# A decoder layer on one core: gate products as two fp32r passes, and one tile's expert search ahead of the others

## The chip, the cores and the metric

The kernel runs on one core of one Trainium2 chip. The metric is the device time of one execution in microseconds (us); smaller is better. The time before is the median of three executions.

## What is computed

One decoder layer on 512 tokens of width 1024: a gated convolution beside a gated linear recurrence, a cross-attention into 256 memory tokens, and a channel mixer that looks up experts by product keys (PEER). The change is in the last part:

```python
q = (tokens @ w_query).reshape(Ntok, PEER_HEADS, 2, PEER_DK)
s = jnp.einsum('nhpd,hpkd->nhpk', q, sub_keys).astype(jnp.float32)
s_top, i_top = lax.top_k(s, K)                       # K = 16 of 128 keys, twice per head
cand = (s_top[:, :, 0, :, None] + s_top[:, :, 1, None, :]).reshape(Ntok, PEER_HEADS, K * K)
best, pos = lax.top_k(cand, K)                       # 16 experts per head and token
gate = jax.nn.softmax(best, axis=-1)
...
u = jnp.take(expert_down, idx, axis=0)               # 128 x 128 = 16384 experts
a = jax.nn.gelu(jnp.einsum('nd,nhkd->nhk', xb, u), approximate=False)
v = jnp.take(expert_up, idx, axis=0)
y = jnp.einsum('nhk,nhkd->nd', gb * a, v)
```

## The kernel before

The 512 tokens are four tiles of 128. Everything is written out by hand, engine by engine; semaphores alone set the order between engines, and each engine works through its own list in order. All large products run in fp32r, a form of float32 that TensorE takes in one pass at less precision. To keep the precision, each operand is split into an upper half (rounded to fp32r) and a lower half (the rest), and three products are summed (`three`, lines 1064 to 1066: high by high, low by high, high by low). Plain float32 products need no split.

Weights come in blocks of 128 x 1024 floats (512 KB) through a ring of four slots. SyncE loads a slot when `block_used` says that it is free; ScalarE rounds it to `w_high` (`high`, line 441); GpSimd subtracts to get `w_low` (`low`, line 347); TensorE uses it (`columns`).

The expert search and the experts go as follows:
- Queries (blocks 68 to 83): 16 blocks of `w_query`, each 24 products of 512 columns (all four tiles), then the keys (line 1287), 64 float32 products of 128 columns. Ahead of them the four tiles are normalised and transposed (lines 696, 702, 1050, 435, 709).
- Tile 3 (`ST`, the sparse tile) fetches its 128 experts per token row by row: GpSimd gathers rows of `expert_down` (line 362), VectorE takes the dot products (`dots`, line 865), and later rows of `expert_up` are added in the same manner (lines 394, 982).
- Tiles 0 to 2 (the dense tiles) compute all 16384 hidden values instead: `first_product`, 128 blocks of 24 products with 384 columns, with gelu on ScalarE (line 610) and the result stored to `hid_dram`. A map of gates, zero but for the chosen experts, then multiplies them, and `second_product` goes over all of `expert_up`.
- The top-k runs on VectorE (`top16` and the lines after it): first for tile 3, then for tiles 0, 1, 2. Meanwhile TensorE computes `first_product` blocks ahead: 72 of them (`AHEAD`) before the gate map starts. `TURN_AT` says after which block TensorE transposes a tile's choices (line 1329), `EXP_AT` after which block ScalarE takes the exponentials (line 632).
- The gate map is made in 48 steps of 8 tokens. VectorE writes one-hot matrices (`hots`: line 953 the first, line 959 the second, already multiplied by the gate); TensorE multiplies them, 8 float32 products of 128 columns per step (`gate_step`, line 1301); ScalarE copies the two banks into `stage` (line 648), and every 8 steps 4 MB go to `gate_dram`. TensorE does one `first_product` block ahead of each step. After the 48 steps 8 blocks are left.

## Time and profile before

| | |
|---|---|
| median of 3 executions | 1727.39 us (1723.75 to 1734.52) |
| profiled execution | 1726.1 us, its span 1724.4 us |
| TensorE busy | 1666.0 us, 97% of the span |
| VectorE, ScalarE, GpSimd busy | 1148.7, 723.8 and 833.1 us |
| mean granted TensorE clock | 0.991 |

The profile is of one execution. The span is the time between the first and the last recorded instruction; the execution's own time is 1.7 us longer. Matmuls overlap in the record, so the time that one product costs in a row of them is the distance between two starts, not its duration.

### The profile page before, as it was taken

Reading aid. Unit: us, or ns where it says so; the run is one execution under the profiler, and the core shown is the slowest. Engines: PE = TensorE matmul, PEld = TensorE weight load, DVE = VectorE, ACT = ScalarE, POOL = GpSimd, SP = SyncE. Lnnn points to the kernel's source line nnn. Section 1 sums busy time; section 2 is a strip of 40 time slices with the busy share of each in tenths; the row PEclk is TensorE's granted clock in tenths of the full one; section 3 lists DMA queues with packets and bytes.
Section 4 is the critical chain, followed back from the end, with each engine's and each line's share of the span. In section 5 each row is a group of like instructions: output and inputs, shape, how many; then the busy total and the mean of one; then the engine's idle time right before and its main releaser. Section 6 shows DMA issues by size and latency. Waiting matters only on the chain.

```text
span 1724.4 us, 25526 instructions
## 1 busy us (share of the span) xinstructions
PE 1666.0 (97%) x8649; PEld 1478.4 (86%) x8649; DVE 1148.7 (67%) x2255; ACT 723.8 (42%) x973; POOL 833.1 (48%) x483
## 2 busy tenths in 40 slices
PE   7999999999999999999999999988999999999998
PEld 5788787867789999999999999987788888888886
DVE  4154562131104979989798888854788887887887
ACT  5342433342324445353455555543333333333333
POOL 3362374314343677878666666655333323433340
PEclk9999999999999999999999999998999999999999
DMA  4222243213223578888788999999999999999994
GB/s 171 86 98 74 74 141 115 86 39 114 77 94 96 171 262 285 282 279 281 271 283 312 335 344 341 341 338 374 359 353 360 343 356 350 339 370 342 349 333 153
DMA packets 150697, 421.26 MB, mean 244 GB/s; under 512 B 14576, under 2 KB 71920, under 8 KB 149744
## 3 DMA queue, kind: packets, MB, share of 16 engines
q1 hardware_dynamic: 93472, 232.29, 39.7%
q0 software_dynamic: 36864, 134.23, 21.5%
q10 hardware_dynamic: 20304, 54.04, 8.0%
q8 instruction: 27, 0.44, 0.1%
q14 instruction: 30, 0.25, 0.0%
HBM read 368.08 MB, written 52.43 MB: 244 GB/s over the span
## 4 chain that ended last, share of the span: by engine, by line
PE 81%; DMA 7%; DVE 5%; ACT 2%; issue 2%; POOL 2%; ACTq 0%; SPq 0%; DVEq 0%; POOLq 0%
PE psum L1064 25%; PE psum L1065 24%; PE psum L1066 24%; DMA arena<-down_rows,kept 4%; PE psum L1301 3%; POOL w_low L347 2%; DMA arena<-hid_dram 1%; DMA arena<-up_in 1%; DVE arena L959 1%; PE psum L1268 1%; PE psum L1287 1%; DVE hT_low L779 1%; DVE hT_high L778 1%; DMA kept<-down_in 1%; PE psum L1244 1%
## 5 line engine op out<-in xcount | busy, mean ns | idle before, releaser
L347 POOL TENSOR_TENSOR w_low<-kept,w_high 128x1024 fp32r<-128x1024 f32 x212 | 520.3, 2456 | 496.5 <-ACT w_high L441 495.9
L1064 PE MATMUL psum<-hT_high,w_high 128*128 128x384 f32 (+1 forms) x1408 | 502.7, 357 | 12.3 <-POOL w_low L347 8.0
L1065 PE MATMUL psum<-hT_low,w_high 128*128 128x384 f32 (+1 forms) x1408 | 494.8, 351 | 0.0
L1066 PE MATMUL psum<-hT_high,w_low 128*128 128x384 f32 (+1 forms) x1408 | 494.8, 351 | 0.0
L441 ACT ACTIVATE w_high<-kept 128x1024 fp32r<-128x1024 f32 x212 | 224.7, 1061 | 203.3 <-DMA kept<-front_w 76.7
L1064 PE MATMUL psum<-up_high,wgt_high 128*128 128x512 f32 x768 | 300.6, 391 | 7.9 <-DVE wgt_low L995 7.6
L1065 PE MATMUL psum<-up_low,wgt_high 128*128 128x512 f32 x768 | 299.8, 390 | 0.0
L1066 PE MATMUL psum<-up_high,wgt_low 128*128 128x512 f32 x768 | 299.7, 390 | 0.0
L1064 PEld LDWEIGHTS psum<-hT_high,w_high 128*128 128x128 f32 x1408 | 266.7, 189 | 30.2 <-POOL w_low L347 9.7
L1066 PEld LDWEIGHTS psum<-hT_high,w_low 128*128 128x128 f32 x1408 | 266.2, 189 | 15.5
L1065 PEld LDWEIGHTS psum<-hT_low,w_high 128*128 128x128 f32 x1408 | 266.6, 189 | 14.8 <-issue 0.5
L445 ACT ACTIVATE up_high<-arena 128x1024 fp32r<-128x1024 f32 x128 | 135.9, 1062 | 325.1 <-DMA arena<-up_in 319.6
L865 DVE CUSTOM_DVE_ANT_0 arena<-arena,psum 128x1024 f32<-128x1024 f32 x128 | 153.3, 1211 | 77.4 <-DMA arena<-down_rows,kept 77.4
L974 DVE TENSOR_TENSOR up_low<-arena,up_high 128x1024 fp32r<-128x1024 f32 x128 | 156.6, 1223 | 56.5 <-ACT up_high L445 55.5
L1064 PEld LDWEIGHTS psum<-up_high,wgt_high 128*128 128x128 f32 x768 | 144.7, 188 | 41.4 <-issue 11.5
L394 POOL DMA_INDIRECT kept<-up_in,kept x64 | 90.7, 1417 | 167.2 <-DVE kept L982 151.4
L1066 PEld LDWEIGHTS psum<-up_high,wgt_low 128*128 128x128 f32 x768 | 144.7, 188 | 30.2
L1065 PEld LDWEIGHTS psum<-up_low,wgt_high 128*128 128x128 f32 x768 | 144.7, 188 | 29.6
L394 POOL DMA_INDIRECT arena<-up_in,kept x64 | 92.9, 1452 | 154.5 <-DVE kept L982 153.3
L610 ACT ACTIVATE arena<-psum 128x384 f32<-128x384 f32 x128 | 62.8, 491 | 200.2 <-PE psum L1066 195.2
L362 POOL DMA_INDIRECT arena<-down_rows,kept x128 | 125.1, 978 | 26.7 <-issue 16.0
L959 DVE TENSOR_SCALAR arena<-psum,arena 128x128 f32<-128x128 f32 x384 | 126.5, 402 | 0.0
(185 smaller groups left out, 1931.1 us busy)
## 6 DMA issues: line engine op xcount, KB each, us to landing
kept<-down_in SPq DMA_DIRECT2D x128, 512.0 KB, 5.0
arena<-up_in SPq DMA_DIRECT2D x128, 512.0 KB, 6.1
kept<-front_w SPq DMA_DIRECT2D x84, 512.0 KB, 3.2
hid_dram<-arena ACTq DMA_DIRECT2D x128, 192.0 KB, 4.7
gate_dram<-arena ACTq DMA_DIRECT2D x6, 4096.0 KB, 15.3
arena<-gate_dram SPq DMA_DIRECT2D x32, 768.0 KB, 7.6
arena<-hid_dram SPq DMA_DIRECT2D x128, 192.0 KB, 7.1
kept<-x_in ACTq DMA_DIRECT2D x4, 512.0 KB, 5.2
```

The source lines that it names most:

```text
L347: nc.gpsimd.tensor_tensor(w_low[:, s, :], ring[:, s, :], w_hi[:, s, :].bitcast(F32), ALU.subtract).then_inc(low_ready, 1)
L362: nc.gpsimd.indirect_dma_start(ring[slot], None, down_rows, bass.IndirectOffsetOnAxis(idx3[:, k:k + 1].bitcast(U32), 0))\
L394: nc.gpsimd.indirect_dma_start(rows_c[k % RING_C], None, up_rows, bass.IndirectOffsetOnAxis(idx3[:, k:k + 1].bitcast(U32), 0))\
L441: nc.scalar.activation(w_hi[:, s, :], ring[:, s, :], ACT.Copy).then_inc(high_ready, 1)
L445: nc.scalar.activation(up_hi[:, s, :], uraw[:, s, :], ACT.Copy).then_inc(up_high, 1)
L610: nc.scalar.activation(hid[s % 2], psum[:, 4 + s % 2, 0:DN], ACT.Gelu).then_inc(gelu_out, 1)
L865: nc.vector.tensor_tensor_reduce(ring[slot], ring[slot], h_row, 1.0, 0.0, ALU.mult, ALU.add, dot3[:, k:k + 1]).then_inc(dot_done, 1)
L959: ins = nc.vector.tensor_scalar(hot[:, s, 1, j % TB * P:(j % TB + 1) * P], iota_ps, hkT[:, 1, j:j + 1], hkT[:, 2, j:j + 1], ALU.is_equal, ...
L974: nc.vector.tensor_tensor(up_lo[:, s, :], uraw[:, s, :], up_hi[:, s, :].bitcast(F32), ALU.subtract).then_inc(up_low, 1)
L1064: nc.tensor.matmul(out, lhs[0], rhs[0], start=first, stop=False)
L1065: nc.tensor.matmul(out, lhs[0], rhs[1], start=False, stop=False)
L1066: return nc.tensor.matmul(out, lhs[1], rhs[0], start=False, stop=last)
```

## The change

Two things are changed, and some counts with them.

The gate map: the second one-hot matrix is still multiplied by the gate, but is written as fp32r, so it holds the gate's upper half. ScalarE makes a third matrix from it with the ratio of lower to upper half (`hot_lows`, eight scaled copies of 128 x 128 per step), and each float32 product becomes two fp32r products that add up in one bank. The rings of one-hot matrices go from 3 to 2. ScalarE copies the result to `stage` in another order of its elements: the writes go in runs of 4, the reads from PSUM at a stride. VectorE computes the ratio for each dense tile in five small operations.

The sparse tile: its residual, norm and transposes come first; its queries are 16 blocks of 8 plain float32 products of 128 columns, straight from the ring with no halves. The 16 blocks are then loaded a second time and used for the three dense tiles, 24 products of 384 columns each. The sparse tile's keys come behind the first of these blocks, and its top-k runs on VectorE during the others. `AHEAD` goes from 72 to 60, so 20 blocks are left behind the gate steps. The dots in a step go from 2 and 1 alternating to 1.

```diff
+RAW0, RAW = 68, 16
+USED = FRONT + RAW
-EXP_AT = (12, 28, 48, 68)
-TURN_AT = (12, 36, 56, 72)
+EXP_AT = (16, 36, 56)
+TURN_AT = (20, 40, 60)
-HOTS = 3
+HOTS = 2
-DOTS_STEP = (2, 1, 2, 1, 2, 1)
+DOTS_STEP = (1, 1, 1, 1, 1, 1)
-FIRST_GATHER = 18
+FIRST_GATHER = 4
...
@@ scalar, in a gate step @@
+            def hot_lows(n, s):
+                act.wait_ge(hot_ready, n + 1)
+                for j in range(TB):
+                    ins = nc.scalar.activation(hot[:, s, 2, j * P:(j + 1) * P], hot[:, s, 1, j * P:(j + 1) * P].bitcast(F32),
+                                               ACT.Copy, scale=hkT[:, 3, n * TB + j:n * TB + j + 1])
+                ins.then_inc(hot_low, 1)
...
             for n in range(STEPS):
+                hot_lows(n, n % HOTS)
                 early_at(AHEAD + n)
...
-                        stage[:, c % 2, :, m % 16 * 4:(m % 16 + 1) * 4].rearrange("p i n -> p n i"),
-                        psum[:, m % 3, :].rearrange("p (n i) -> p n i", i=P), ACT.Copy).then_inc(gate_out, 1)
+                        stage[:, c % 2, :, m % 16 * 4:(m % 16 + 1) * 4],
+                        psum[:, m % 3, :].rearrange("p (n i) -> p i n", n=4), ACT.Copy).then_inc(gate_out, 1)
@@ vector @@
+            dve.wait_ge(ks_out, 4)
+            choose(score[:, ST, :], sparse_k, 0, (0, 0, 0, 0), (0, 0, 0, 0), 0, 0)
+            nc.vector.scalar_tensor_tensor(idx3.bitcast(U32), sparse_k.hk[:, 0, :], float(NK), sparse_k.hk[:, 1, :],
+                                           ALU.mult, ALU.add).then_inc(idx_ready, 1)
...
+            for n in range(DT):
+                kd = choose(score[:, n, :], dense_k, kd, DOTS_SCORES[n], DOTS_CAND, DOTS_HOT[n], n)
+                gates_of(dense_k, hk[:, 2, :], n + 2)
+                step(nc.vector.tensor_copy(ghigh, hk[:, 2, :]))
+                step(nc.vector.tensor_tensor(glow, hk[:, 2, :], ghigh.bitcast(F32), ALU.subtract))
+                step(nc.vector.tensor_scalar(gden, ghigh.bitcast(F32), 1e-30, None, ALU.max))
+                step(nc.vector.reciprocal(gden, gden))
+                nc.vector.tensor_tensor(hk[:, 3, :], glow, gden, ALU.mult).then_inc(hk_ready, 1)
@@ tensor @@
-            turned_columns(ffnn, 68, 4)
+            for q in range(RAW):
+                pe.wait_ge(wt[q % 4], 16 * ((RAW0 + q) // 4 + 1))
+                for k in range(KC):
+                    ins = nc.tensor.matmul(psum[:, 2 + q // 4 % 2, q % 4 * P:(q % 4 + 1) * P], ring[:, q % 4, k * P:(k + 1) * P],
+                                           hT_s[:, k, :], start=(k == 0), stop=(k == KC - 1), skip_group_check=True)
+                ins.then_inc(block_used, 1)
...
             def gate_step(n, h):
-                pe.wait_ge(hot_ready, n + 1)
+                pe.wait_ge(hot_low, n + 1)
...
-                        ins = nc.tensor.matmul(psum[:, (2 * h + m) % 3, j % 4 * P:(j % 4 + 1) * P],
-                                               hot[:, h % HOTS, 1, j * P:(j + 1) * P], hot[:, h % HOTS, 0, j * P:(j + 1) * P],
-                                               start=True, stop=True)
+                        nc.tensor.matmul(gate, hot[:, h % HOTS, 1, j * P:(j + 1) * P], hot[:, h % HOTS, 0, j * P:(j + 1) * P],
+                                         start=True, stop=False, skip_group_check=True)
+                        ins = nc.tensor.matmul(gate, hot[:, h % HOTS, 2, j * P:(j + 1) * P],
+                                               hot[:, h % HOTS, 0, j * P:(j + 1) * P], start=False, stop=True,
+                                               skip_group_check=True)
```

On TensorE, the head of the queries before: all four tiles are transposed (`ffn_h` counts normalised tiles), then the first block follows at 512 columns.

```order
L1050 MATMUL psum<-kept,arena 128x128 [waits block_used,ffn_h]
L1050 MATMUL psum<-kept,arena 128x128 x3
L1050 MATMUL psum<-kept,arena 128x128 [waits ffn_h]
...
L1064 MATMUL psum<-hT_high,w_high 128x512 [waits ffn_ready,low_ready,ffn_h]
L1065 MATMUL psum<-hT_low,w_high 128x512
```

The same place in the changed kernel: line 1352 transposes the sparse tile alone, line 1362 is its queries (one block in two rows), and behind 16 such blocks the dense tiles' first block begins.

```order
L1352 MATMUL psum<-kept,arena 128x128 [waits block_used,ffn_sparse_h]
L1352 MATMUL psum<-kept,arena 128x128 x7
L1362 MATMUL psum<-arena,kept 128x128 [waits ffn_sparse_ready,weight_slot0]
L1362 MATMUL psum<-arena,kept 128x128 [waits ffn_sparse_ready] x7
L1362 MATMUL psum<-arena,kept 128x128 [waits weight_slot1]
L1362 MATMUL psum<-arena,kept 128x128 x7
...
L1142 MATMUL psum<-hT_high,w_high 128x384 [waits low_ready,ffn_ready]
L1143 MATMUL psum<-hT_low,w_high 128x384
L1144 MATMUL psum<-hT_high,w_low 128x384
```

The raw blocks wait for the loads alone (`weight_slot`), the dense ones for ScalarE's and GpSimd's halves as well.

On ScalarE, one gate step before: gelu and its store, the two copies to `stage`, the rounding of the block that comes two blocks later.

```order
L610 ACTIVATE arena<-psum 128x384 [waits hid_stored0,block_used]
L612 DMA hid_dram<-arena 128x384 [waits gelu_out]
L648 ACTIVATE arena<-psum 128x4x128 [waits gate_done] x2
L441 ACTIVATE w_high<-kept 128x1024 [waits weight_slot3,block_used]
```

One gate step on ScalarE in the changed kernel:

```order
L667 ACTIVATE arena<-psum 128x384 [waits hid_stored0,block_used]
L669 DMA hid_dram<-arena 128x384 [waits gelu_out]
L708 ACTIVATE arena<-psum 128x128x4 [waits gate_done] x2
L695 ACTIVATE hot<-hot,arena 128x128 [waits hot_ready]
L695 ACTIVATE hot<-hot,arena 128x128 x7
L459 ACTIVATE w_high<-kept 128x1024 [waits weight_slot3,block_used]
```

The eight scaled copies stand between the copies to `stage` and the rounding, and they wait for VectorE's one-hots.

## Rows read from the trace of the kernel before

**Rows 1.** The page: busy time by engine, and TensorE's granted clock in 40 slices.
```profile
PE 1666.0 (97%) x8649; PEld 1478.4 (86%) x8649; DVE 1148.7 (67%) x2255; ACT 723.8 (42%) x973; POOL 833.1 (48%) x483
...
PEclk9999999999999999999999999998999999999999
```

**Rows 2.** Who waited for whom: us in total, times, longest us.
```profile
DVE arena L865 <- DMA arena<-down_rows,kept: 77.4, 22, 11.5
...
PE psum L1301 <- DVE arena L959: 8.1, 7, 2.0
```

**Rows 3.** TensorE in order of time, queries: start, duration (us), operation.
```profile
430.63 1.32 PE L1050 MATMUL psum<-kept,arena 128*128 128x128 f32 x8 [1.54 <-DVE arena L696]
...
435.08 0.77 PE L1064 MATMUL psum<-hT_high,w_high 128*128 128x512 f32 x1 [1.01 <-DVE hT_low L709]
...
526.04 14.45 PE L1287 MATMUL psum<-arena 128*128 128x128 f32 x128
540.25 0.42 PE L1064 MATMUL psum<-hT_high,w_high 128*128 128x384 f32 x1
```

**Rows 4.** TensorE in order of time: fp32r products of 256, then of 384 columns.
```profile
232.75 0.28 PE L1065 MATMUL psum<-memT_low,w_high 128*128 128x256 f32 x1
...
237.19 0.28 PE L1066 MATMUL psum<-memT_high,w_low 128*128 128x256 f32 x1
...
861.58 0.34 PE L1066 MATMUL psum<-hT_high,w_low 128*128 128x384 f32 x1
...
865.25 0.33 PE L1066 MATMUL psum<-hT_high,w_low 128*128 128x384 f32 x1
```

**Rows 5.** TensorE in order of time: plain float32 products of 128 and 64 columns.
```profile
167.17 0.44 PE L1180 MATMUL psum<-arena 128*128 128x128 f32 x2
167.45 0.56 PE L1185 MATMUL psum<-arena 128*128 128x64 f32 x4
167.84 0.44 PE L1180 MATMUL psum<-arena 128*128 128x128 f32 x2
```

**Rows 6.** TensorE's weight loads in order of time, behind an idle array.
```profile
267.52 0.19 PEld L1064 LDWEIGHTS psum<-w_high,hT_high 128*128 128x128 f32 x1 [0.70 <-issue]
267.62 0.19 PEld L1065 LDWEIGHTS psum<-w_low,hT_high 128*128 128x128 f32 x1
```

**Rows 7.** Groups by line: busy us, mean ns, idle before and its releaser.
```profile
L1301 PE MATMUL psum<-arena 128*128 128x128 f32 x768 | 94.2, 276 | 8.1 <-DVE arena L959 8.1
```

**Rows 8.** VectorE in order of time: top-k of tile 3, first dots, first one-hots.
```profile
541.16 0.29 DVE L891 COPY psum<-kept 128x128 f32<-128x128 f32 x1 [97.79 <-ACT arena L600]
...
595.25 1.23 DVE L946 TENSOR_TENSOR psum<-arena 128x1024 f32<-128x1024 f32 x1
...
618.09 1.22 DVE L865 CUSTOM_DVE_ANT_0 arena<-arena,psum 128x1024 f32<-128x1024 f32 x1 [6.69 <-DMA arena<-down_rows,kept]
...
847.24 1.22 DVE L953 TENSOR_TENSOR arena<-arena,psum 128x1024 f32<-128x1024 f32 x1 [7.08 <-ACT arena L637]
```

**Rows 9.** One source line: ns min/median/max, first and last start, forms.
```profile
L940 DVE TENSOR_TENSOR arena<-arena x3: 1016/1695/2674, 679.3 to 838.5; 128x128 f32<-128x128 f32 x3
...
L632 ACT ACTIVATE arena<-arena x4: 310/310/312, 592.7 to 831.5; 128x128 f32<-128x128 f32 x4
```

**Rows 10.** ScalarE in order of time, one gate step.
```profile
883.46 0.49 ACT L610 ACTIVATE arena<-psum 128x384 f32<-128x384 f32 x1 [2.21 <-PE psum L1066]
...
884.36 2.03 ACT L648 ACTIVATE arena<-psum 128x512 f32<-128x512 f32 x2 [0.41 <-PE psum L1301]
886.18 1.08 ACT L441 ACTIVATE w_high<-kept 128x1024 fp32r<-128x1024 f32 x1
889.40 0.49 ACT L610 ACTIVATE arena<-psum 128x384 f32<-128x384 f32 x1 [2.15 <-PE psum L1066]
```

**Rows 11.** DMA issues: KB each, us to landing.
```profile
kept<-front_w SPq DMA_DIRECT2D x84, 512.0 KB, 3.2
```

More of the change, by code:

```diff
@@ L87, in build @@
             w_half, up_half = (w_hi, w_low), (up_hi, up_lo)
+        with ExitStack() as over:
+            over.enter_context(nc.sbuf_tensor("pad_hot", [P, 92 * KB], F32))
+            hot = over.enter_context(nc.sbuf_tensor("hot", [P, HOTS, 3, TB * P], F32R))
         kept = ctx.enter_context(nc.sbuf_tensor("kept", [P, 44 * KB], F32))
@@ L366, in _ @@
             k = 0
-            for i in range(16, AHEAD + 2):
+            for i in range(4, AHEAD + 2):
                 low(FRONT + i, i % 4)
@@ new lines, in _ @@
+            step(nc.vector.tensor_tensor(h_row, hn[:, ST, :], ffn_row, ALU.mult))
+            dve.wait_ge(pk_out, 4 * DT)
+            kd = 0
+            for n in range(DT):
+                kd = choose(score[:, n, :], dense_k, kd, DOTS_SCORES[n], DOTS_CAND, DOTS_HOT[n], n)
[5 more added lines that the diff above has]
+                nc.vector.tensor_tensor(hk[:, 3, :], glow, gden, ALU.mult).then_inc(hk_ready, 1)
@@ L1095, in rows @@
                 if tile_done is not None:
-                    steps = [(j, n) for n in range(len(banks)) for j in range(2)]
+                    steps = [(j, n) for n in order for j in range(2)]
                 for j, n in steps:
@@ L1100, in rows @@
                                 k0 + j == 0, k0 + j == KC - 1)
-                    if tile_done is not None and j == 1 and n < len(banks) - 1:
+                    if tile_done is not None and j == 1 and n != order[-1]:
                         ins.then_inc(tile_done, 1)
@@ L1209, in _, with product @@
                 keys(32 + b, b)
-            def product(lhs, b0, done, first, parts=None):
+            def product(lhs, b0, done, first, order, parts=None):
                 for hf in range(2):
```

358 lines of the change are left out of this document (212 added, 146 removed).

## The prediction

> **What bounds the kernel now.** I read the page's busy times first [rows 1]. TensorE is busy for 1666.0 of 1724.4 us and its granted clock is full in nearly every slice; the next engine, VectorE, stands at 67%. The 58 us that TensorE sits idle is all that better order could ever win. So I ask two things of every edit: what it adds to or takes from TensorE's own list, and whether it opens a gap there. The waits [rows 2] show how small the gaps around the change are: in the whole gate stage TensorE waited 8.1 us for one-hots, though VectorE waited 77.4 us for gathered rows. That the sparse tile's top-k (55 us on VectorE, from 541.16 to 596.5 [rows 8]) now runs during the queries gains nothing by itself, since TensorE worked through it.
>
> The sums are made against the profiled execution, 1726.1 us (span 1724.4 plus 1.7 outside); the median of the three runs is 1727.4, so the two agree.
>
> **Prices of a product.** In a row of products the price is the distance between starts. fp32r: 37 products of 256 columns take 237.19 - 232.75 = 4.44 us, 0.120 each; 21 of 384 columns take 865.25 - 861.58 = 3.67 us, 0.175 each [rows 4]. The line through both gives 0.230 at 512 columns and 0.065 at 128. Plain float32: each product is two records, and six records stand in 167.84 - 167.17 = 0.67 us, 0.112 each, although four of the six have only 64 columns [rows 5]. So the price there does not fall with the columns; something per record holds it at 0.112. A candidate: behind an idle array, with nothing to wait for, two fp32r weight loads start 0.10 us apart [rows 6]. Each product has its own weight load, so I read a load of 128 columns as taking 0.10 to 0.11 us, for fp32r too.
>
> **Queries.** Before, TensorE's part runs from 429.1 (430.63 less the wait of 1.54) to 540.25, 111.2 us: waits of 1.54 and 1.01, transposes, 16 blocks, and the keys from 526.04 [rows 3]. The blocks at 0.230 x 24 x 16 make 88.3 us of the 91.0 between 435.08 and 526.04; the rest is the slow clock behind the wait (the first product there lasts 0.77 us), which I take to come again. After: sparse queries 16 x 8 products x 2 records x 0.112 = 28.7 us; dense queries 16 x 24 x 0.175 = 67.2. Keys and transposes are as many as before. 28.7 + 67.2 - 88.3 = **+7.6 us**, all on the path.
>
> The gaps at that place: the sparse tile's norm now starts while the last three tiles' products still run, which can save most of the 2.6 us of waits [rows 3]. But behind the last raw block TensorE needs halves of the first dense block. Its slot comes free three raw blocks (3 x 16 x 0.112 = 5.4 us) before, and the load takes 3.2 [rows 11], the rounding 1.1 [rows 10] and GpSimd's low half about twice that, some 6.7 in all with 1.3 to 3 us of waiting. Together **+1 us**, between -2 and +5. The raw blocks also need 512 KB every 1.8 us. A slot is refilled in 3.2 us [rows 11] and has 5.4, so I take 0; if transfers that overlap take twice as long, a slot is 1 us late in each round of four blocks and the end is +8.
>
> **Gate products.** Before: 768 records [rows 7], 16 a step, 16 x 0.112 = 1.79 us; with the 24 products of a block 4.20 this makes the step of 889.40 - 883.46 = 5.94 that ScalarE's rows show [rows 10]. After: 16 fp32r products of 128 columns a step. No row has fp32r below 256 columns. The array time would fall, but the number of weight loads stays at 16. With the load as the floor the price is between 0.107 and the 0.120 of 256 columns; I take 0.115, near the float32 row, as the overhead of an fp32r product looks a little larger: 16 x 0.003 x 48 = **+2 us**, between -4 and +6. That is the step on which most hangs: the expected gain of one pass instead of two for each record is not there, because the loads bind.
>
> **ScalarE in a step.** It was idle 2.15 of 5.94 us [rows 10] and gets eight scaled copies of 128 columns. From below, 1.08 us per 1024 columns gives 0.13 each, 1.1 in all; from above, the 0.31 of a lone operation of that size [rows 9] gives 2.5. The two copies to `stage` take 2.03 us for 2 x 512 elements [rows 10]; they write at a stride now and will write runs of four, so I expect them cheaper, not dearer. I take 1.6, and the engine is then full at some 90%. It costs nothing while this cover holds; each 0.1 us beyond it costs 4.8 us over 48 steps.
>
> **VectorE ahead of the gates.** Before, three dense tiles took from 596.5 to 840.2 (847.24 less 7.08), 243.7 us, with waits for rows such as the 6.69 in it [rows 8]. New are 15 small operations; one of that size took 0.3 us alone and 1.0 to 2.7 us beside GpSimd [rows 9]; at 0.75 they make 11, and gathers that start earlier give 2 back: 253. TensorE has 60 blocks x 4.2 = 252 us there, so the two finish together, where VectorE had been 7 us early. Then the first step waits for a copy, one-hots and now scaled copies (0.6 + 3.8 + 2) with one block of 4.2 beside it. I take **+3 us** for both, between 0 and +19.
>
> **Waits in the gate stage.** VectorE has 1 dot a step for 1.5, so 5.1 us of work in 5.9; and four gathered rows last four steps (24 us) instead of 2.7 (16). Most of the 8.1 us goes [rows 2]: **-5 us**, between -8 and 0. Two one-hot buffers instead of three cost nothing while VectorE has this slack. The 20 blocks left behind the steps are the same work in another place.
>
> **The sum.** 1726.1 + 7.6 + 1 + 2 + 3 - 5 = **1735 us**; its bounds are 1726 + 7.6 - 2 - 4 - 8 = 1720 and 1726 + 7.6 + 5 + 8 + 6 + 19 = 1772, the last with all of them at once.
>
> **Rivals.** *Faster: the loads hide.* If the distance of the two loads is not the load's, the price falls on the line to 0.065, and 16 products cost 1.05 us. The step cannot go below VectorE's 5.1, so it ends near 5.25: 0.7 x 48 = 33 us less than before, 35 less than forecast, 1700 us. For it: the line through two widths is straight to 256 columns. Against it: the 64-column row and the two loads. The Trainium skill (TensorE: Matmul & The Clock Gate, section on the back-to-back issue gap) gives about 81 ns a product for a stream of loads and products at 128 columns; by that the gates would be an estimated 23 us cheaper than before. Its page FP8 and Floating Point Precision (section TensorE Precision Notes) counts four passes for true FP32 and a plain truncation for the reduced form, which speaks for this rival as well; no row here shows it at 128 columns.
>
> *Slower: a narrow fp32r product costs as much as a full float32 one.* The kernel used fp32r only from 256 columns up, and nothing shows that the one-pass rate holds below. If each of the 16 then costs the two records of a float32 product, 0.224, a step grows by 16 x 0.112 = 1.79 us: 86 us over 48 steps, 1735 - 2 + 86 = 1819. It decides as soon as the price is over 0.15 (+30 us).
>
> *Slower: ScalarE becomes the bound.* If the scaled copies cost over 0.27 each, or the strided read from PSUM makes the `stage` copies dearer, the step is ScalarE's. At 0.3 to 1.0 us over, 1750 to 1783. In the same group stands VectorE coming late at each of the three turns.
>
> *It does nothing.* The sparse tile's move would only matter if its top-k had been on the path; that is in the forecast.
>
> **How the numbers follow.** The forecast has 0.60, the hidden loads 0.14, the dear narrow product 0.12, ScalarE or VectorE as the bound 0.14. About 1% (17 us) is what a measurement of this kernel can tell from no change: 1710 to 1745. The forecast lies within it for 0.48 of its 0.60, above for 0.10, below for 0.02. The hidden loads are faster for 0.12 and land within for 0.02; the other two are slower. Faster 0.14, same 0.50, slower 0.36. For 8 in 10 the range runs from 1702, most of the way to the hidden loads, to 1780, which takes in nearly all of the ScalarE case and leaves the dear product out.
>
> **What would show it.** Starts of the gate products 0.11 to 0.12 us apart, with weight loads back to back, and a step of about 6.0 us; 0.065 or 0.22 would be the first two rivals. TensorE idle before the step's fp32r products with ScalarE's copies as releaser would be the third. The queries should take 28.7 and 67 us, with a gap of 1 to 3 us between. The waits for one-hots should be gone but for the first.

## The result, and the profile after

| | before | changed |
|---|---|---|
| median of four timed runs, same chip, us | 1725.57 | 1751.37 |
| ratio | 1 | 1.014, 95% interval 1.009 to 1.019 |
| profiled execution, us | 1726.1 | 1749.39 |
| its span, us | 1724.4 | 1747.7 |
| TensorE's mean granted clock in it | 0.991 | 0.989 |

The change costs 26 us by the medians and 23.3 us by the two profiled executions. It is slower by 1.4%, clear of the noise of these runs. The page of the changed kernel, busy time by engine and the granted clock, answers to [rows 1]:

```profile
PE 1679.7 (96%) x8908; PEld 1504.2 (86%) x8908; DVE 1164.7 (67%) x2268; ACT 785.0 (45%) x1356; POOL 828.7 (47%) x483
...
PEclk9999999999999999999999999899999999999999
```

TensorE is busy for 13.7 us more and stands 68.0 us instead of 58.4. Who TensorE waited for (us in total, times, longest us), where [rows 2] had 8.1 us for VectorE's one-hots:

```profile
PE psum L1142 <- POOL w_low L367: 14.7, 13, 7.5
PE psum L1142 <- DVE wgt_low L1073: 12.3, 11, 4.9
...
PE psum L1410 <- ACT hot L695: 7.8, 6, 3.0
```

The one-hots are gone from the list. In their place stand ScalarE's scaled copies with nearly the same sum, and GpSimd's low halves with 14.7 us, where the same wait of before had 8.0. Not all of the 14.7 us lies behind the gate steps: the same view of the stretch behind them alone gives, before and then changed,

```profile
PE psum L1064 <- POOL w_low L347: 4.8, 1, 4.8
```

```profile
PE psum L1142 <- POOL w_low L367: 10.4, 10, 7.5
```

To place the 23.3 us I cut both executions at the same events of TensorE's list. The moved blocks are taken out at 4.17 us each, TensorE's pace for 24 products of 384 columns:

| stretch | before | changed | change |
|---|---|---|---|
| start to the end of attention | 429.1 | 425.3 | -3.8 |
| queries and keys, to the first first-product block | 111.15 | 118.25 | +7.1 |
| to the first gate product, without its 72 (60) blocks | 10.7 | 11.4 | +0.7 |
| first to last gate product, 48 steps | 290.0 | 292.7 | +2.7 |
| to the last first product, without its 8 (20) blocks | 6.7 | 15.7 | +9.0 |
| wait before the second product | 5.0 | 5.1 | +0.1 |
| second product to the end | 538.1 | 545.7 | +7.6 |

The first and the last stretch run the same instructions in both kernels. Over all fourteen profiled kernels of this study the first ends between 423.7 and 429.1 us, and the last takes 538.1 to 548.9 us; a repeat of nearly the old kernel (e6 below) has 546.6 there. The profiled execution of before has the longest first stretch of the fourteen and the shortest last one. So I take those two rows as scatter, and three rows are left to explain: +7.1, +2.7 against a forecast of -3, and +9.0 against a forecast of nothing.

**Queries.** TensorE in order of time at the turn from the sparse queries to the dense ones, for [rows 3]:

```profile
457.28 0.94 PE L1362 MATMUL psum<-arena,kept 128*128 128x128 f32 x7
461.00 0.41 PE L1142 MATMUL psum<-hT_high,w_high 128*128 128x384 f32 x1 [2.78 <-POOL w_low L367]
...
532.80 11.00 PE L1395 MATMUL psum<-arena 128*128 128x128 f32 x96
```

The 256 records of line 1362 start between 426.6 and 457.9, with 24 records of the other tiles' transposes among them (2.6 us), and behind them TensorE waits 2.78 us for GpSimd's low half of the first dense block.

**Gate products.** TensorE in order of time, the first of one step's eight pairs:

```profile
887.41 0.22 PE L1410 MATMUL psum<-hot 128*128 128x128 f32 x1
887.47 0.27 PE L1412 MATMUL psum<-hot 128*128 128x128 f32 x1
887.58 0.27 PE L1410 MATMUL psum<-hot 128*128 128x128 f32 x1
887.69 0.28 PE L1412 MATMUL psum<-hot 128*128 128x128 f32 x1
887.80 0.28 PE L1410 MATMUL psum<-hot 128*128 128x128 f32 x1
```

They start 0.11 us apart, as the float32 records of [rows 7] did (0.112). ScalarE in the same step, for [rows 10]:

```profile
881.64 0.49 ACT L667 ACTIVATE arena<-psum 128x384 f32<-128x384 f32 x1 [1.36 <-PE psum L1144]
...
882.55 0.60 ACT L708 ACTIVATE arena<-psum 128x512 f32<-128x512 f32 x1 [0.41 <-PE psum L1412]
883.38 0.60 ACT L708 ACTIVATE arena<-psum 128x512 f32<-128x512 f32 x1 [0.23 <-PE psum L1412]
883.88 2.44 ACT L695 ACTIVATE hot<-hot,arena 128x128 fp32r<-128x128 f32 x8
886.22 1.05 ACT L459 ACTIVATE w_high<-kept 128x1024 fp32r<-128x1024 f32 x1
887.60 0.49 ACT L667 ACTIVATE arena<-psum 128x384 f32<-128x384 f32 x1 [0.33 <-PE psum L1144]
```

The step takes 887.60 - 881.64 = 5.96 us; by the starts of TensorE's gate products an undisturbed step of before takes 5.95. The eight scaled copies take 2.44 us, and in front of the next gelu ScalarE waits 0.33 us where it waited 2.15 before. The two copies to `stage` cost 0.60 each where they cost about 1.0 before.

That is the quiet step. Five steps behind the stores of the gates are not quiet. ScalarE in order of time at one of them, and TensorE:

```profile
918.51 1.06 ACT L459 ACTIVATE w_high<-kept 128x1024 fp32r<-128x1024 f32 x1 [2.40 <-DMA kept<-down_in]
920.01 0.49 ACT L667 ACTIVATE arena<-psum 128x384 f32<-128x384 f32 x1 [0.44 <-DMA hid_dram<-arena]
...
921.89 2.44 ACT L695 ACTIVATE hot<-hot,arena 128x128 fp32r<-128x128 f32 x8
...
924.46 0.32 PE L1410 MATMUL psum<-hot 128*128 128x128 f32 x1 [1.13 <-ACT hot L695]
```

VectorE had its one-hots ready: in the whole gate stage of the changed kernel ScalarE never waited for them. It came late to the scaled copies because its own list stood for a block and for a small store of `hid_dram`, which had been issued at 906.08 behind the 4 MB store and landed 13.9 us later.

**Behind the steps.** GpSimd in order of time:

```profile
1125.81 2.39 POOL L367 TENSOR_TENSOR w_low<-kept,w_high 128x1024 fp32r<-128x1024 f32 x1
1128.36 0.95 POOL L382 DMA_INDIRECT arena<-down_rows,kept  x1 [0.16 <-issue]
1129.61 0.94 POOL L382 DMA_INDIRECT arena<-down_rows,kept  x1 [0.31 <-DVE kept L930]
1130.57 2.42 POOL L367 TENSOR_TENSOR w_low<-kept,w_high 128x1024 fp32r<-128x1024 f32 x1
1133.15 0.95 POOL L382 DMA_INDIRECT arena<-down_rows,kept  x1 [0.16 <-issue]
```

A low half and two gathers, one behind the other on one engine, take 1130.57 - 1125.81 = 4.76 us, and TensorE eats a block in 4.17. Shortly before, behind the sixth store, the same list stands still:

```profile
1105.78 2.41 POOL L367 TENSOR_TENSOR w_low<-kept,w_high 128x1024 fp32r<-128x1024 f32 x1
1116.09 0.95 POOL L382 DMA_INDIRECT arena<-down_rows,kept  x1 [7.90 <-DVE kept L930]
...
1120.04 2.36 POOL L367 TENSOR_TENSOR w_low<-kept,w_high 128x1024 fp32r<-128x1024 f32 x1
```

A gather waits there for the buffer of a row that VectorE has not summed yet, because VectorE stood 14.2 us, until 1114.59, for a row to land. The rounded half of the next block is ready at 1116.4, but its low half starts only at 1120.04, behind the gathers.

### The profile page after: what moved, and what is told of

Same layout as the page of the kernel before. It is cut to its first block, busy times and chain, and to the rows that moved or that the text cites. A ratio compares the mean times of both kernels' runs of the same rounds, so it can differ in the third digit from the quotient of the medians.

```text
span 1747.7 us, 26507 instructions
## 1 busy us (share of the span) xinstructions
PE 1679.7 (96%) x8908; PEld 1504.2 (86%) x8908; DVE 1164.7 (67%) x2268; ACT 785.0 (45%) x1356; POOL 828.7 (47%) x483
## 4 chain that ended last, share of the span: by engine, by line
PE 51%; issue 20%; POOL 12%; DMA 11%; ACT 3%; DVE 2%; SPq 0%; ACTq 0%; POOLq 0%; DVEq 0%
PE psum L1142 16%; PE psum L1144 16%; PE psum L1143 16%; POOL w_low L367 10%; DMA arena<-hid_dram 4%; DMA hid_dram<-arena 3%; DMA arena<-down_rows,kept 2%; PE psum L1410 2%; PE psum L1412 2%; POOL arena L382 2%; ACT hot L695 1%; DMA arena<-up_in 1%; DMA kept<-down_in 1%; PE psum L1395 1%; ACT w_high L459 1%
## 5 line engine op out<-in xcount | busy, mean ns | idle before, releaser
L1142 PE MATMUL psum<-hT_high,w_high 128*128 128x384 f32 (+1 forms) x1408 | 495.9, 352 | 18.1 <-POOL w_low L367 14.7
L1144 PE MATMUL psum<-hT_high,w_low 128*128 128x384 f32 (+1 forms) x1408 | 488.5, 347 | 0.0
L1143 PE MATMUL psum<-hT_low,w_high 128*128 128x384 f32 (+1 forms) x1408 | 488.3, 347 | 0.0
L382 POOL DMA_INDIRECT arena<-down_rows,kept x128 | 125.4, 979 | 34.7 <-issue 12.8
L1037 DVE TENSOR_SCALAR hot<-psum,arena 128x128 fp32r<-128x128 f32 x384 | 126.6, 402 | 0.0
```

Source lines behind the costliest of these rows:

```text
L382: nc.gpsimd.indirect_dma_start(ring[slot], None, down_rows, bass.IndirectOffsetOnAxis(idx3[:, k:k + 1].bitcast(U32), 0))\
L1037: ins = nc.vector.tensor_scalar(hot[:, s, 1, j % TB * P:(j % TB + 1) * P], iota_ps, hkT[:, 1, j:j + 1], hkT[:, 2, j:j + 1], ALU.is_equal, ...
L1142: nc.tensor.matmul(out, lhs[0], rhs[0], start=first, stop=False)
L1143: nc.tensor.matmul(out, lhs[0], rhs[1], start=False, stop=False)
L1144: return nc.tensor.matmul(out, lhs[1], rhs[0], start=False, stop=last)
```

## The experiments

All ratios are to the kernel before, run on the same chip beside it; its median there was 1723.0 to 1725.9 us. "Stage" is the time from the first to the last gate product; "clock" is TensorE's mean granted clock in it, 1.00 being full speed. e4, e6, e8 and e11 leave the lower half of the gates out, e9 and e10 leave out parts of the map; they are there to measure, not to use.

| run | median us | ratio, 95% | stage us | clock |
|---|---|---|---|---|
| before | 1725.6 | 1 | 290.0 | 1.00 |
| changed | 1751.4 | 1.014 (1.009 to 1.019) | 292.7 | 0.98 |
| e1_gates_only | 1761.9 | 1.022 (1.018 to 1.026) | 324.1 | 0.93 |
| e2_sparse_only | 1729.4 | 1.003 (1.000 to 1.005) | 281.5 | 1.00 |
| e3_gathers_earlier | 1764.5 | 1.024 (1.020 to 1.027) | 326.9 | 0.93 |
| e4_upper_alone | 1734.4 | 1.006 (1.004 to 1.009) | 276.6 | 0.94 |
| e5_two_buffers | 1723.0 | 0.998 (0.996 to 1.000) | 289.7 | 1.00 |
| e6_two_fp32r | 1727.3 | 1.001 (0.998 to 1.003) | 290.6 | 1.00 |
| e7_paced | 1733.7 | 1.005 (1.003 to 1.007) | 286.6 | 1.00 |
| e8_upper_three_buffers | 1717.0 | 0.994 (0.992 to 0.997) | 262.4 | 0.96 |
| e9_small_stores | 1713.3 | 0.994 (0.992 to 0.997) | 283.9 | 0.99 |
| e10_half_columns | 1743.9 | 1.010 (1.007 to 1.014) | 293.3 | 0.94 |
| e11_upper_dots_sooner | 1705.9 | 0.988 (0.985 to 0.991) | 260.3 | 0.97 |
| e12_spread_stores | 1730.5 | 1.003 (1.001 to 1.005) | 284.5 | 0.99 |

### e1: the gate part alone

The kernel before with the two fp32r passes, the scaled copies on ScalarE, two one-hot buffers and the new order of the copies to `stage`; the sparse tile and the dots stay where they were.

```diff
-HOTS = 3
+HOTS = 2
...
+                hot_lows(n, n % HOTS)
...
-                pe.wait_ge(hot_ready, n + 1)
+                pe.wait_ge(hot_low, n + 1)
...
```

> The kernel before with the gate part alone: two fp32r passes, the scaled copies on ScalarE, two one-hot buffers, the other order of the copies to stage; queries, top-k order, 72 blocks ahead and 8 behind stay as they were. The theory (the weight loads keep 16 products at 0.11 us each, so the gate part moves nothing; the loss comes from the queries and from GpSimd in the blocks behind the gates) expects within 5 us of the kernel before, with a step of about 6.0 us. The rival (the gate part costs the time, by its third engine in the chain and the lost buffer) expects 12 to 25 us more than before.

It came to 1761.9 us, 36 us over before. My theory of a part that costs at most a few us fell. Who TensorE waited for:

```profile
PE psum L1322 <- ACT hot L649: 27.2, 6, 5.5
```

Six waits only, 55 us apart: one before the first step, and one for each of the first five groups of eight steps, at the fourth step behind the 4 MB store of the group's gates. ScalarE, VectorE and TensorE in order of time at one of them:

```profile
907.61 2.44 ACT L649 ACTIVATE hot<-hot,arena 128x128 fp32r<-128x128 f32 x8
913.09 1.06 ACT L446 ACTIVATE w_high<-kept 128x1024 fp32r<-128x1024 f32 x1 [3.04 <-DMA kept<-down_in]
914.52 0.49 ACT L615 ACTIVATE arena<-psum 128x384 f32<-128x384 f32 x1 [0.37 <-DMA hid_dram<-arena]
...
920.22 2.44 ACT L649 ACTIVATE hot<-hot,arena 128x128 fp32r<-128x128 f32 x8 [3.71 <-DVE hot L979]
...
912.29 1.22 DVE L879 CUSTOM_DVE_ANT_0 arena<-arena,psum 128x1024 f32<-128x1024 f32 x1 [7.35 <-DMA arena<-down_rows,kept]
...
915.27 1.22 DVE L879 CUSTOM_DVE_ANT_0 arena<-arena,psum 128x1024 f32<-128x1024 f32 x1 [1.75 <-DMA arena<-down_rows,kept]
...
917.55 2.64 DVE L979 TENSOR_SCALAR hot<-psum,arena 128x128 fp32r<-128x128 f32 x8
...
922.80 0.47 PE L1322 MATMUL psum<-hot 128*128 128x128 f32 x1 [5.53 <-ACT hot L649]
923.06 0.41 PE L1324 MATMUL psum<-hot 128*128 128x128 f32 x1
923.28 0.41 PE L1322 MATMUL psum<-hot 128*128 128x128 f32 x1
```

While the store runs (15.0 us to landing by the DMA table), VectorE stands 7.35 us for one gathered row and 1.75 for the next (13.0 us from issue to landing in the chain of waits). The one-hots come behind these two sums in VectorE's list, and end at 920.2. The scaled copies need another 2.4 us, and only then may TensorE start. It has stood 5.53 us, and the products behind the wait start 0.21 us apart instead of 0.11: the clock is at its lower level, 1.2 GHz (granted 0.50 from 922.8 to 929.5). The stage adds up: from the first to the last gate product it holds 47 steps of 5.96 and the 1.6 us of the last step's products, 281.8 us; the five waits inside it are 24.2, and 18 are left for products at the lower clock, in all 324.1 us.

### e2: the sparse tile's move alone

The changed kernel with the float32 gate products, their one wait, three buffers and the order of the copies to `stage` of before; the new order of the queries, the later gathers and the 20 blocks behind the steps stay.

```diff
-HOTS = 2
+HOTS = 3
...
-                hot_lows(n, n % HOTS)
...
-                pe.wait_ge(hot_low, n + 1)
+                pe.wait_ge(hot_ready, n + 1)
...
```

> The changed kernel with the gates as they were before: float32 products, three one-hot buffers, no scaled copies; the sparse tile ahead, 60 blocks ahead and 20 behind stay. The theory expects 18 to 25 us more than the kernel before, as the full change; the rival that blames the gates expects 5 to 10 us more than before (the queries alone).

It came to 1729.4, 3.5 us over before. That is under both expectations, the theory's 18 to 25 us and the rival's 5 to 10, so the move alone is not what costs. Its stage takes 281.5 us without one wait of TensorE, and at the full clock; TensorE and the others by stretch (us; busy us and instructions of each engine; clock; DMA share; GB/s), the stage and the blocks behind it:

```profile
798.10:1079.60 281.50, 281.50 (x1895) 281.21 (x1896) 234.82 (x526) 159.76 (x189) 161.54 (x98) 1.00 0.81 290
1079.60:1177.30 97.70, 88.18 (x483) 84.54 (x481) 35.86 (x59) 32.02 (x41) 68.57 (x45) 0.97 0.99 369
```

The stage gains 8.5 us; the stretch behind it holds 20 blocks in 97.7 us, where 83.4 would do, and so gives 7.6 of them back against before.

The two parts alone cost 36 and 4 us, together 26. They aren't independent: the move brings one row a step instead of one and a half, and that takes most of the gate part's waits away (27.2 us in e1, 7.8 in the changed kernel). The next run shows it.

### e3: the changed kernel with the rows of before

```diff
-DOTS_STEP = (1, 1, 1, 1, 1, 1)
+DOTS_STEP = (2, 1, 2, 1, 2, 1)
```

> The changed kernel with 2, 1, 2, 1 dots and gathers in a gate step in place of 1, so that 7 rows in place of 30 are left for the 20 blocks behind the gates. The theory (there GpSimd needs 2.4 us for a low half and 1.25 us for each of two gathers, 4.8 us a block, where TensorE needs 4.2) expects these blocks to come at 4.2 us and a time 5 to 10 us under the changed kernel's. The rival (VectorE, with 1.5 dots a step and one buffer less, then holds the gate steps) expects the gain to be lost there: no change or slower.

```profile
PE psum L1410 <- ACT hot L695: 28.2, 6, 5.6
```

The run took 1764.5 us, 13 more than the changed kernel, where the theory expected 5 to 10 less; the rival was right. The waits rose from 7.8 to 28.2 us, and the stage from 292.7 to 326.9. The tail, the blocks behind the steps, shrank from 99.1 to 89.5 us, so on that stretch the theory held: its waits for low halves fell from 10.4 to 4.2 us, and the rest is time at the lower clock. So the slower pace of rows is worth 34 us in the stage and costs 10 behind it.

### e4: the upper half alone

In the changed kernel the second product of each pair is left out; the copies still run, and the gates' lower half is missing from the output.

```diff
-                        nc.tensor.matmul(gate, hot[:, h % HOTS, 1, j * P:(j + 1) * P], hot[:, h % HOTS, 0, j * P:(j + 1) * P],
-                                         start=True, stop=False, skip_group_check=True)
-                        ins = nc.tensor.matmul(gate, hot[:, h % HOTS, 2, j * P:(j + 1) * P],
-                                               hot[:, h % HOTS, 0, j * P:(j + 1) * P], start=False, stop=True,
-                                               skip_group_check=True)
+                        ins = nc.tensor.matmul(gate, hot[:, h % HOTS, 1, j * P:(j + 1) * P], hot[:, h % HOTS, 0, j * P:(j + 1) * P],
+                                               start=True, stop=True, skip_group_check=True)
```

> The changed kernel with one fp32r product per token in place of two: the lower half of the gate is left out of the products (its copies are still made). If the weight loads are the price, 8 loads less a step save 0.89 us, and the step shrinks until VectorE's 5.1 us hold it: 35 to 42 us less than the changed kernel. If the array's columns were the price and the loads hidden, the same products would save half as much or less.

384 products fewer at 0.11 are 42 us; the time fell by 17 (the stage by 16.1) and not by the 35 to 42 expected. The waits for ScalarE's copies went from 7.8 to 24.7 us and the clock from 0.98 to 0.94. They stand behind the stores again, 3.5 to 4.9 us each, so much of what TensorE saves is waited away. That a shorter step leaves ScalarE less time to make up a delay is my reading of it.

### e5 and e6: two buffers alone, the product form alone

e5 is the kernel before with one line changed:

```diff
-HOTS = 3
+HOTS = 2
```

> The kernel before with two one-hot buffers in place of three, and nothing else. In the gates-only run TensorE waited 27 us at six steps behind the 4 MB stores and the clock fell behind each wait. If the lost buffer is the cause (VectorE waits for gathered rows and has one step less in hand), this costs most of those 36 us: 20 to 35 us over the kernel before. If the new link through ScalarE is the cause (one-hots, then scaled copies, then the products), this stays within 5 us of before.

e6 is the kernel before with two fp32r products of the upper half for each float32 one, three buffers, no scaled copies; the lower half is missing from the gates.

```diff
+            hot = over.enter_context(nc.sbuf_tensor("hot", [P, HOTS, 2, TB * P], F32R))
...
+                        for _ in range(2):
                             ins = nc.tensor.matmul(psum[:, (2 * h + m) % 3, j % 4 * P:(j % 4 + 1) * P],
```

> The kernel before with each float32 gate product replaced by two fp32r products of the upper half alone (the second overwrites the first; the lower half of the gate is left out), three buffers and no scaled copies. If the weight loads set the price of both forms, the gate step stays at 5.9 to 6.0 us and the time within 3 us of before. If the one-pass form were cheaper at 128 columns it would be up to 35 us faster, if dearer up to 86 us slower.

Neither costs anything: 0.998 and 1.001, with 7.7 and 8.1 us of waits for one-hots, as before. e6's group of gate products beside [rows 7] (busy us, mean ns of one, idle before):

```profile
L1304 PE MATMUL psum<-hot 128*128 128x128 f32 x768 | 91.8, 272 | 8.1 <-DVE hot L961 8.1
```

Both came as expected. What is left as the cause in e1 is the link that neither of them has: one-hots, then ScalarE's copies, then TensorE, with two buffers. Whether the link alone would do it stays open. Three buffers with the link weren't tried: the memory has no room for them beside `stage` and the rows.

### e7: rows paced between the two

```diff
-DOTS_STEP = (1, 1, 1, 1, 1, 1)
+DOTS_STEP = (2, 1, 1, 1, 1, 1)
...
-                for _ in range(DOTS_STEP[i % PER_GROUP] if i < DURING else 2):
+                for _ in range(DOTS_STEP[i % PER_GROUP] if i < DURING else 1 + (i % 4 == 0)):
```

> The sparse tile ahead with float32 gates and three buffers (as in the sparse-only run), with the gathers spread: 7 in 6 gate steps, 5 in 4 blocks behind them, in place of 1 and 2. The theory (behind the gates GpSimd needs 4.8 us a block with two gathers) expects these blocks at 4.2 us and 4 to 8 us less than the sparse-only run, 1722 to 1726. The rival (the blocks behind the gates wait for loads that the last store delays, whatever GpSimd does) expects no change.

On e2's base; it came to 1733.7. The tail behind the steps shrank by 7 us, to 90.7, the stage grew by 5, and the second product took 548.9, the longest of all runs. Expected were 1722 to 1726; against e2's 1729.4 there is no gain, as the rival had it, though not for its reason, since the tail did answer to the pace. In both runs that move rows from the tail into the stage, e3 and this one, the stage grew.

### e8 and e11: what the link and the second pass cost together

e8 is the changed kernel with one fp32r product a pair (the lower half is missing from the gates), three buffers, no copies, and two and one row in turn behind the steps; e11 is e8 with two rows a block there, as the changed kernel has. The edit of e8 in part, without the products:

```diff
-HOTS = 2
+HOTS = 3
...
-                hot_lows(n, n % HOTS)
...
-                pe.wait_ge(hot_low, n + 1)
+                pe.wait_ge(hot_ready, n + 1)
...
-                for _ in range(DOTS_STEP[i % PER_GROUP] if i < DURING else 2):
+                for _ in range(DOTS_STEP[i % PER_GROUP] if i < DURING else 2 - i % 2):
```

> The sparse tile ahead, one fp32r product per token with the upper half of the gate (the lower half is left out), three buffers, no scaled copies, the copies to stage in the new order, 1 gather a step and 2, 1, 2, 1 behind the gates. If buffers and the ScalarE link held up the run with the upper half alone in two buffers (1734 us), this one goes at VectorE's 5.1 to 5.2 us a step: 35 us under the sparse-only run, 1690 to 1700. If the DMA stores hold it whatever the buffers are, it stays above 1715.

> e8_upper_three_buffers with two rows a block behind the gate steps, as the changed kernel has them, instead of two and one in turn. In e8 the last row's sum ended 2 us behind the last first product, the loads of gates and hid that wait for it took 14 us more, and TensorE stood 20.65 us and then ran 20.5 us at the lower clock. Theory: the wait falls to 1 to 5 us and the slow clock behind it to 2 to 5 us, about 24 us less; GpSimd's pace of 4.8 us a block on 10 blocks gives 4 to 7 back: 1697 to 1704 us. Rival (GpSimd holds the rows' gathers, not their pacing): the rows end no earlier and the time stays at 1712 to 1718.

e8 came to 1717.0 instead of 1690 to 1700. Its stage is short (262.4), but TensorE then stood before the second product:

```profile
PE psum L1140 <- DVE wgt_low L1071: 26.1, 8, 20.7
```

The chain of waits names it: the last gathered rows land at 1156.3, their sum ends at 1157.6, and only then does SyncE's list come to the loads of `hid_dram` and gates, of which one takes 14.05 us. With the rows sooner (e11) that wait is 4.9 us again, as in before, and the time 1705.9 (expected 1697 to 1704), 1.2% under before and the fastest here, without the lower half of the gates; GpSimd's pace costs it 7.6 us in the tail, 99.8 us against e8's 92.2. Its stage is not free of waits either:

```profile
PE psum L1408 <- ACT arena L707: 11.2, 5, 2.7
```

These are the copies to `stage`. At one of the five ScalarE's list had stood 7.54 us for a block and 1.06 for a store of `hid_dram`, behind the 4 MB store. With a step of 5.1 us even that shows without the link; with 5.95 in e2 nothing did.

### e9 and e12: the store

e9 is e1 with stores of 1 MB instead of 4 MB, three quarters of the gates being left out.

```diff
-                    act.dma_start(gate_dram[:, c, :], stage[:, c % 2].rearrange("p i n -> p (i n)"))\
+                    act.dma_start(gate_dram[:, c, 0:NK * CH // 4], stage[:, c % 2].rearrange("p i n -> p (i n)")[:, 0:NK * CH // 4])\
...
-                sp.dma_start(gates[s], gate_dram[:, :, bass.ds(i * CH, GT * CH)])
+                sp.dma_start(gates[s], gate_dram[:, :, 0:GT * CH])
```

> The kernel before with the gate part alone (as e1_gates_only), but each of the six stores of a group of gates writes a quarter of its columns (1 MB instead of 4 MB), and the second product loads its gates from that quarter, the same number of bytes; three quarters of the gates are never stored. Nothing else changes on any engine. Theory (the store delays rows and blocks, and ScalarE's list hands the delay to TensorE through the scaled copies): of the 27.2 us of waits for scaled copies in e1 at most 8 stay, the time at the lower clock falls from 69 us to 30 to 45, and the time from 1762 to 1727 to 1742 us. Rival (the scaled copies with two buffers are too slow by themselves, store or not): waits stay above 20 us and the time between 1755 and 1765.

e12 stores everything again, in four parts of 1 MB that are issued two steps apart.

```diff
-                if k == CH // TB - 1:
-                    act.wait_ge(gate_out, 2 * (n + 1) + 3)
-                    act.dma_start(gate_dram[:, c, :], stage[:, c % 2].rearrange("p i n -> p (i n)"))\
+                if c and k % 2 == 0:
+                    store_part(c - 1, k // 2)
+            act.wait_ge(gate_out, 2 * STEPS + 3)
+            for q in range(4):
+                store_part(DCH - 1, q)
```

> e1_gates_only with all gates stored, but each 4 MB store of a group is cut in four of 1 MB, which ScalarE issues at every second step of the next group (12 us apart) instead of all at once; the last group's four come at once behind the steps. The bytes are e1's. Theory (what e1 lost was the burst, not the bytes and not the scaled copies themselves): waits for scaled copies fall from 27.2 us to under 6, TensorE's mean granted clock in the gate stage from 0.93 to 0.98 or more, the stage from 324 to 284 to 290 us, and the time to 1712 to 1726, a gain on the kernel before if under 1718. Rival (the 24 MB collide with rows and blocks whenever they come, and e9 was fast because 18 MB were left out): waits of 10 us and more in many small pieces, the time between 1735 and 1760.

e9 came to 1713.3 us against e1's 1761.9, below the 1727 to 1742 expected, and 0.6% under before. Who waited, e9 first, then e12:

```profile
PE psum L1322 <- ACT hot L649: 3.2, 2, 3.0
```

```profile
PE psum L1091 <- ACT arena L615: 12.8, 1, 12.8
...
PE psum L1329 <- ACT hot L649: 3.4, 3, 3.0
```

In both hardly more than the wait before the first step is left, and the stage is 283.9 and 284.5 us. e12 has e1's bytes, copies, buffers and rows, and its stage is 39.6 us shorter: in e1's stage the burst was what the link turned into waits, and neither the bytes nor the copies by themselves cost that. In whole times e12 is still 0.3% over before. The changed kernel itself was not run with its stores in parts. My time for e12 was still wrong, 1730.5 instead of 1712 to 1726. The last group's four parts come at once behind the steps, and ScalarE in order of time shows what that does:

```profile
1136.18 3.20 ACTq L656 DMA_DIRECT2D gate_dram<-arena  x4
...
1164.48 0.49 ACT L615 ACTIVATE arena<-psum 128x384 f32<-128x384 f32 x1 [13.15 <-DMA hid_dram<-arena]
```

The small store of `hid_dram` issued at 1141.01 behind them on the same queue landed 23.4 us later; gelu waited for its buffer, and TensorE for gelu, 12.8 us. The stretch behind the steps took 48.7 us against e1's 39.8. The other part of the miss is the second product, with 544.2 us against 538.9 in e9; I can't give a cause for that beyond its scatter. Spreading the last group as well wasn't tried.

### e10: half the columns

In the changed kernel the first four of a step's eight pairs multiply 64 moving columns instead of 128, the other four load 64 stationary columns; half of the gates is left out.

```diff
+                        mc, sc = (P // 2, P) if m == 0 else (P, P // 2)
+                        for i in (1, 2):
+                            ins = nc.tensor.matmul(gate[0:sc, 0:mc], hot[:, h % HOTS, i, j * P:j * P + sc],
+                                                   hot[:, h % HOTS, 0, j * P:j * P + mc], start=(i == 1), stop=(i == 2),
+                                                   skip_group_check=True)
```

> The changed kernel in which the first four of a step's pairs multiply 64 moving columns instead of 128 and the other four load 64 stationary columns instead of 128; the weights' rows, the number of products and all else stay, and half of the gate columns is left out. Theory (the weight load holds the price, per product): starts stay 0.11 us apart in the first eight products of a step; the other eight stay at 0.11 or, if a load's time goes with its columns, fall to some 0.06 to 0.08; the time stays at 1745 to 1754, or falls by at most 8 x 0.04 x 48 = 15 us in the second case. Rival (the columns hold it): the first eight fall to 0.05 to 0.08, and the time by 15 to 20 us.

The gate products of one step in two windows, of the eight with 64 moving columns and of the eight with 64 stationary ones (us, products and weight loads with their busy time, clock, DMA share, GB/s):

```profile
864.72:865.62 0.90, 0.87 (x9) 0.90 (x10) 1.00 0.99 392
865.62:866.05 0.43, 0.43 (x9) 0.43 (x8) 1.00 1.06 428
```

A window counts what reaches into it, so each count is one or two too high. Eight in 0.90 us are 0.11 each: half the moving columns change nothing. Eight in 0.43 to 0.48 us are 0.06 each: half the stationary columns halve the price. So the stationary columns hold it. Half of them are half a weight load and also half as many output rows; that it is the load is my reading, with the two loads of [rows 6] that start 0.10 us apart behind an idle array. A step is then 864.75 - 859.18 = 5.57 us, 0.39 less, which over 48 steps would be 19 us. The stage did not get shorter (293.3), as shorter steps were waited away in e4: the waits for scaled copies rose from 7.8 to 16.4 us, and the clock fell to 0.94. The 7 us that the time fell against the changed kernel are no more than the scatter of the unchanged stretches.

## Why the prediction held, and where it missed

The range held, and 1751 is 16 us over the forecast of 1735. Of my three cases it is "slower", above the 1745 up to which I called it the same; I had given that 0.36. Two steps were wrong. That the time stayed this near is partly luck: the change slows the rows to one a step, which I had priced as relief for VectorE alone, and that also kept the gate part's stalls small. With the rows of before the same kernel takes 1764.5 us (e3), and the gate part alone 1761.9 (e1).

**Gate products, +2: held.** 0.11 us apart, and 47 undisturbed steps are 0.5 us dearer; e6 puts the form's cost at nothing measurable, and e10 shows the stationary columns as what sets it. So the two rivals on the price fall, the hidden loads and the dear narrow product. The 81 ns of the Trainium skill (TensorE: Matmul & The Clock Gate, section on the back-to-back issue gap) stand beside 0.11 us measured here, and the measurement decides.

**Queries, +7.6 and +1: held.** Measured +7.1 with the gap of 2.78 us included; the slots of raw blocks caused no wait.

**VectorE ahead of the gates, +3: held in kind.** Measured +0.7. The first gate wait was 2.95 us and the waits at the turns small.

**"ScalarE in a step", 0: the cover wasn't enough.** The eight copies take 2.44 us, near the upper bound of 2.5 and not the 1.6 taken. That is 0.305 each, over the 0.27 from which I called the step ScalarE's; it isn't, because the two copies to `stage` gave 0.8 us back. I weighed all this against the idle time of an undisturbed step, and there it does fit. The step that failed was to treat ScalarE's slack in a quiet step as the only condition. The copies also lengthen the chain from VectorE to TensorE by 2.4 us, and they stand in a list that itself waits for blocks and stores. In e1 the late row of VectorE came through the link; in the changed kernel ScalarE's own list did it. The rival "ScalarE becomes the bound" was right about the releaser of the waits and wrong about their form: no step is ScalarE's, but one in eight is.

**Waits in the gate stage, -5: the sign was wrong.** e2 shows that the reasoning on rows was right: its stage gained 8.5 us, beyond even the bound of -8. In the changed kernel the waits inside the stage did fall, but only from 7.1 to 4.9 us (the first wait of each list, 1.0 and 2.95 us, lies ahead of it). What turned the sign is the speed behind them: before lost 1.6 us by slower products there, the changed kernel 6.0, most of it at the lower clock, for which the forecast had no term. The stage is +2.7 where the two terms gave -3. "Two one-hot buffers instead of three cost nothing" is true by itself (e5), but whether they still do with the link was not separated.

**"The 20 blocks left behind the steps are the same work in another place": wrong, +9.0.** During a step GpSimd has 5.96 us for a low half and one gather; behind the steps it has 4.17 for a low half and two, and needs 4.76 as long as rows are left. The waits for low halves there went from 4.8 to 10.4 us, 5.6 of the 9.0: 2.7 by the first one, 7.5 us behind the sixth store, where GpSimd's list stood for a row buffer, and 2.9 by nine small ones, its pace. The lower clock behind the first wait gives the rest (0.05 of 99.1 us against 0.04 of 40.1, 3.4 us more). e3 and e7, with fewer rows there, have 89.5 and 90.7 us for the same blocks.

**Size.** The terms of the forecast make +8.6. The tail adds 9.0, the stage 5.7, queries and the stretch ahead of the gates take back 3.8 of what I gave them; the unchanged stretches add 3.8 in the profiled execution. That makes the 23.3 us between the profiled executions. A stall behind a store was in no rival with its own price; e12's stage, 39.6 us shorter than e1's, shows what it can cost.

## What to carry to other kernels

When an engine is put in between two others, count its work twice: against its idle time in a quiet step, and as length of the chain at the moment at which both engines ahead of it wait for memory. A store of several MB in one piece is such a moment. Cut in parts issued some steps apart it cost e12's stage 40 us less than e1's; the last store needs the same, by e12's tail, though no run here did that. And when work is moved out of a stage, divide each engine's share of it by the time that the new place has for a block, not only TensorE's.

## What the runs showed of the hardware

In a row of fp32r products the distance between starts goes by the stationary columns when these are many and the moving ones few: 0.11 us with 128 stationary and either 128 or 64 moving columns, 0.06 with 64 stationary and 128 moving.

A 4 MB store (15 us to landing) makes other transfers late. A gathered row, 6.3 us at the median of before, took 13.0 us in e1 and 18.5 in the changed kernel behind it; a 192 KB store of `hid_dram`, 4.7 us at the median, took 13.9 in the changed kernel, and 23.4 in e12 behind four stores of 1 MB issued at once. Single stores of 1 MB landed in 5.5 us (e9) and 7.0 (e12, median of 24), and in the gate stage TensorE hardly waited.

ScalarE's copy to `stage` takes 0.60 us for 512 columns when it reads PSUM with a stride and writes runs of four, against about 1.0 when it read in order and wrote with a stride. Which of the two does it wasn't separated.

The clock falls behind short waits too, though not at once and not always. Behind e1's five waits of 4.38 to 5.53 us the gate products start 0.21 to 0.22 us apart from the first one on, at 1.2 GHz. Behind the wait of 1.13 us in the changed kernel (at 924.46) they start 0.11 us apart, and the lower clock comes with the next block (busy us of PE, weight loads, VectorE, ScalarE and GpSimd; clock; DMA share; GB/s):

```profile
923.50:926.20 2.70, 1.74 (x16) 1.75 (x16) 0.55 (x2) 2.29 (x6) 0.85 (x1) 1.00 0.85 231
926.20:930.40 4.20, 4.20 (x18) 4.20 (x17) 3.86 (x10) 4.20 (x11) 2.48 (x2) 0.59 0.59 186
```

That step took 7.65 us instead of 5.96. The same happened behind the wait of 1.31 us at 873.8, but not behind one of 1.31 us in the kernel before, where the next step took 6.07. What decides between them no run here shows. The lower clock cost e1 18 us on 24.2 us of waits.
